# Gated down product: four of six rounds as seven half-size products; the gated entry in another row order

## What is computed

```
x = layer_norm(ALPHA * x + merged @ w_o, ln1_g, ln1_b)              # 1024 x 1024
hid = silu(x @ w_gate) * (x @ w_up)                                 # 1024 x 2816
x = layer_norm(ALPHA * x + hid @ w_down, ln2_g, ln2_b)              # 2816 x 1024
```

## Time and profile before

| | before |
|---|---|
| median of 3 runs | 2722.92 us (2715.91 to 2723.53) |
| the profiled execution | 2724.81 us, span 2722.9 us |
| matmuls (PE instructions) | 14122 |
| PE busy, DVE busy | 2608.5 us, 1756.0 us |
| mean granted clock of TensorE | 0.981 |

### The profile page before, as it was taken

The page is one execution under the profiler, slowest core; times in us unless marked ns, Lnnn a source line. Parts: engine busy times, 40 slices in busy tenths (PEclk is TensorE's granted clock), DMA queues, the critical chain, the costliest instruction groups (busy, mean ns, idle before and its releaser), DMA issues. The chain is left out here.

```text
span 2722.9 us, 35770 instructions
## 1 busy us (share of the span) xinstructions
PE 2608.5 (96%) x14122; PEld 2082.8 (76%) x14122; DVE 1756.0 (64%) x2663; ACT 902.2 (33%) x1578; POOL 479.2 (18%) x237
## 2 busy tenths in 40 slices
PE   7999999999899999999999999999969999999998
PEld 5875558884478887788888888868967888887887
DVE  5894997772667668999683355323276666666446
ACT  4334443420354544333231222232143322323121
POOL 1212644420000003333211121234200000000000
PEclk9999998989999999999999999999989999999999
DMA  4011032230133336333221222252322322235221
GB/s 160 31 63 67 31 124 94 95 125 23 62 109 113 110 111 243 105 102 108 89 90 51 75 87 69 71 208 70 124 78 64 91 77 86 78 93 224 76 110 62
DMA packets 192757, 262.22 MB, mean 96 GB/s; under 512 B 15952, under 2 KB 121808, under 8 KB 192208
## 3 DMA queue, kind: packets, MB, share of 16 engines
q1 hardware_dynamic: 192592, 259.95, 28.2%
HBM read 196.80 MB, written 61.93 MB: 95 GB/s over the span
## 5 line engine op out<-in xcount | busy, mean ns | idle before, releaser
L1341 PE MATMUL ps<-gl_t,gl_slot 128*128 128x512 f32 x1056 | 243.0, 389 | 0.0
L1341 PEld LDWEIGHTS ps<-gl_t,gl_slot 128*128 128x128 f32 x1056 | 198.3, 188 | 41.3
L1341 PE MATMUL ps<-gl_b,gl_slot 128*128 128x512 f32 x768 | 182.4, 395 | 18.4 <-DVE gl_slot L3912 18.4
L1341 PEld LDWEIGHTS ps<-gl_b,gl_slot 128*128 128x128 f32 x768 | 146.7, 191 | 49.9 <-issue 14.4
L1341 PE MATMUL ps<-ff_t,slot 128*128 128x512 f32 x768 | 179.2, 393 | 4.4 <-DVE ff_t L3195 4.4
L1341 PE MATMUL ps<-H_hi,tw_hi 128*128 128x512 f32 x448 | 175.6, 392 | 0.0
L1341 PE MATMUL ps<-H_rest,tw_hi 128*128 128x512 f32 x448 | 174.4, 389 | 0.0
L1341 PE MATMUL ps<-H_hi,tw_lo 128*128 128x512 f32 x448 | 174.3, 389 | 0.0
L1341 PEld LDWEIGHTS ps<-ff_t,slot 128*128 128x128 f32 x768 | 145.9, 190 | 35.3 <-DVE ff_t L3195 4.8
L1415 PE MATMUL ps<-wq_raw,H_plain 128*128 128x512 f32 x384 | 166.6, 593 | 2.6 <-ACT sb L2099 2.6
L1349 PE MATMUL ps<-b_hi,a_hi 128*128 128x512 f32 x376 | 147.3, 392 | 5.7 <-DVE sb L3535 3.8
(11 more groups left out here) (459 smaller groups left out, 5997.3 us busy)
## 6 DMA issues: line engine op xcount, KB each, us to landing
wraw<-in_w_ff SPq DMA_DIRECT2D x16, 1024.0 KB, 5.9
ff_raw<-ff_rows SPq DMA_DIRECT2D x8, 2048.0 KB, 8.0
slab_raw<-in_w_ff SPq DMA_DIRECT2D x16, 1024.0 KB, 5.0
ff_rows<-quad SPq DMA_DIRECT2D x61, 256.0 KB, 2.0
traw<-in_w_in SPq DMA_DIRECT2D x28, 512.0 KB, 4.4
wq_raw<-in_w_in SPq DMA_DIRECT2D x6, 2048.0 KB, 9.3
wraw<-in_w_gate SPq DMA_DIRECT2D x22, 512.0 KB, 3.9
wraw<-in_w_up SPq DMA_DIRECT2D x22, 512.0 KB, 5.1
```

The lines of the kernel that those rows point to most:

```text
L1341: mm = nc.tensor.matmul(out_ap, stationary(a, k), moving(c, k), start=(k == 0 and n == 0), stop=(k == kts - 1 and n == 2))
```

## The change

Rounds 1 to 4 of the gated down product (numbered r = 8 to 11 in the shared code) become seven half-size products each, with the functions of the first down product, which now take either stage. Round 0 (two contraction tiles) and the last round keep 16 outputs. DVE's sums t1, t2, t4 and the rests of products 0 and 1 of r = 8 stand among the additions of round 0; POOL makes the left sums of r = 8 and all left rests. The loads change places: the slabs of `w_down` for r = 8 are issued right behind rows 0 to 2 of X, those for r = 9 where those for round 1 stood, and the gain and shift of the last norm behind all of it. The entry's row order becomes 0 4 1 5 2 3 6 7, and the work on a transposed row moves from behind the norm of the row two later into it.

```diff
+LN_ROWS = (0, 4, 1, 5, 2, 3, 6, 7)
...
-            for i in range(GL_ROUNDS - 1):
-                for h in range(2):
-                    pe.wait_ge(v_lo, GL_ITEM_AT[("s", i, 1) if h else ("f", i, 3) if i else ("s", 0, 0)])
-                    for t in DOWN_ROWS:
-                        gl_output(i, h, t)
+            for h in range(2):
+                pe.wait_ge(v_lo, GL_ITEM_AT["s", 0, h])
+                for t in DOWN_ROWS:
+                    b = wait_bank(pe, *gl_down(0, h, t))
+                    split_product(ps[:, b, :], lambda a, k: (hid_lo if a else hid_hi)[:, k, t * P:(t + 1) * P],
+                                  lambda a, k: down_w[h][a][:, k, :], 2).then_inc(full[b], 1)
+            for r, x in GL_SEVENTH_ORDER:
+                seventh(r, x)
             pe.wait_ge(v_lo, GL_ITEM_AT["s", GL_ROUNDS - 1, 1])
...
                 if p == GL_PAIRS - 1 and x == 4:
                     gl_full(sp, p, x)
                     sp.dma_start(X[:, 0:3, :], xln_rows[0:3].rearrange("t p c -> p t c")).then_inc(part_in[0], 16)
+                    for h in range(2):
+                        gl_slab_load(GL_FIRST, h)
             sp.wait_ge(hid_f, 2 * GL_PAIRS - 1)
             sp.dma_start(X[:, 3, :], xln_rows[3]).then_inc(part_in[3], 16)
             for h in range(2):
                 sp.wait_ge(v_lo, GL_ITEM_AT["s", 0, h])
-                gl_slab_load(1, h)
+                gl_slab_load(GL_FIRST + 1, h)
...
             sp.dma_start(X[:, 6:NT, :], xln_rows[6:NT].rearrange("t p c -> p t c")).then_inc(part_in[6], 16)
+            quarter_full(sp, GL_FIRST, 0)
+            gl_hidden_load(GL_FIRST + 1)
+            for r in range(GL_FIRST + 2, GL_LAST + 1):
+                quarter_full(sp, r - 2, 4)
+                gl_slab_load(r, 0)
+                quarter_full(sp, r - 2, 3)
+                gl_slab_load(r, 1)
+                quarter_full(sp, r - 2, 6)
+                gl_hidden_load(r)
...
+            first_left_sums(GL_FIRST)
+            for x in FIRST_SEVEN[:6]:
+                left_rest(GL_FIRST, x)
+            for r in range(GL_FIRST + 1, GL_LAST):
+                later_left_rests(r)
...
-            for q, t in enumerate(MIX_ROWS):
+            for q, t in enumerate(LN_ROWS):
+                behind = LN_ROWS[q - 2] if q > 1 else None
                 merged_drain(t, 1)
                 for h in range(2):
                     wait_drained(dve, *merged("w", t, h))
                 row_mean(t)
+                if q > 1 and behind < 4:
+                    gl_rest_half(behind)
+                if q > 1 and behind >= 4:
+                    gl_term_sums(behind - 4)
+                    gl_rest_terms(behind - 4)
+                if q == NT - 1:
+                    gl_rest_weight(0)
+                    gl_rest_weight(1)
                 row_arg(t, q)
                 row_centred(t, q)
+                if q > 1 and behind >= 4:
+                    gl_rest_second(behind - 4)
                 row_root(t, 1)
                 row_normed(t, q)
-                if q > 1:
-                    gl_rest_turned(q - 2)
...
+            for h in range(2):
+                for t in DOWN_ROWS:
+                    b = wait_full(dve, *gl_down(0, h, t))
+                    xs = X[:, t, 512 * h:512 * h + 512]
+                    if h == 0 and t in (4, 0, 3, 6):
+                        dve.wait_ge(part_in[t], 64)
+                    V.scalar_tensor_tensor(xs, xs, ALPHA, ps[:, b, :], mul, add).then_inc(drained[b], 1)
+                    if (h, t) == (0, 1):
+                        right_sum(GL_FIRST, "t1")
+                    if (h, t) == (0, 3):
+                        right_rest(GL_FIRST, 0)
+                    if (h, t) == (0, 7):
+                        right_sum(GL_FIRST, "t2")
+                    if (h, t) == (1, 5):
+                        right_sum(GL_FIRST, "t4")
+                    if (h, t) == (1, 1):
+                        right_rest(GL_FIRST, 1)
+            first_rounds(GL_FIRST)
+            for r in range(GL_FIRST + 1, GL_LAST):
+                later_rounds(r, gl_last_rest)
+            gl_last_rest("s", 1)
+            quarter_added(GL_LAST - 1, 6)
```

458 lines of the change are left out of this document (257 added, 201 removed).

## The result

The changed kernel takes **2689.12 us** (median of 4 runs, 2687.22 to 2695.23), the kernel before, run beside it, 2720.66 us (2715.91 to 2723.53): a ratio of 0.9892, 95% interval 0.9879 to 0.9904, so 31.5 us or 1.1% faster, well over the 0.3% that a measurement tells. The forecast was 2697.4 (2688 to 2709). The median lies inside the range, 1.1 us above its lower end; the forecast gain was 25.5 us, so the change gave 6 us more than forecast. The other 2.3 us between 2697.4 and 2689.12 come from the kernel before, whose median was 2722.92 when the forecast was made.

A forecast was written before the change was run, and what follows sets the result against it. The prediction took PE's matmuls plus the few places where PE waits as the bound. Its terms, -21.8 for matmuls, +10.1 for start-up and -13.8 for the entry, summed to -25.5 us: median 2697.4 us, range 2688 to 2709.

The forecast's parts named there:

- Fewer matmuls: Four rounds of the gated down product: 168 matmuls each in place of 192, 96 fewer on PE's path, -21.8 us.
- DVE in the four rounds: Gated down product: DVE's 35.4 us a round fit under PE's 38.1, so its added work costs nothing.
- The rule against: DVE and POOL lock a shared SBUF port; six full 2.4 us blocks a round would give 49.8 us, time about 2744.
- rival D: Four rounds: each of POOL's six operations stretches DVE by 2.2 us, DVE becomes the bound, slower at 2739; chance 3%.
- The load of rows 6 and 7: Round 0 of the gated down product: X's load lands 2.6 us later, PE gap 3.7 us, bounds 1.0 and 6.3.
- Before product 1: Gated down product's round 0: DVE's list behind the load delays product 1, gap 2.7 us, bounds 0 and 6.5.
- First of the four rounds: Gated down product's first seven-product round: gaps like the first down product's opening, 4.0 us, bounds 1.5 and 6.
- Clock: Gated down product's start: PE loses 3.4 us to the lower clock level, bounds 0 and 5.2.
- Start-up together: Gated down product: load, product 1, first seven-round and clock sum to 13.7 us against 3.65 before, +10.1 us.
- The entry: Gated entry: new row order and DVE work moved into waits start PE's first term product at 2042.4, not 2056.17, -13.8 us.
- B: Gated down product: the start-up eats the saving, leaving a gain of 1.5 there, time 2707.6 us; chance 11%.
- C: Gated entry gives nothing because PE or ACT, not DVE, holds the rows; only -11.7, time 2711.2 us; chance 5%.

The follow-up runs named there:

- POOL behind: Against the changed kernel, POOL's six rests a round start 1.8 us later in the three later seven-product rounds, none added; 2710.63 us, ratio 0.9968.
- doubled: Against the changed kernel, 17 POOL subtractions of 2.4 us each added in the three later seven-product rounds; 2713.50 us, ratio 0.9975.

## Why the prediction was right, and where it was off

**Fewer matmuls, -21.8.** Right: x14026, and what is left of 229.87 - 217.9 is gaps and clock.

**DVE in the four rounds, nothing.** Right in its result (40.00 of 40 with DVE at 37.00), by luck in its sum. The prediction counted 28 additions and no meeting with POOL, 35.4 us a round. The later round read above has 24 additions (product 6 of a round and product 0 of the next are added up in the same banks and drained once), which is 2.4 us less, and three meetings of 0.65 us, which is 1.9 more: 35.13 measured. The two errors cancel, and so the cover, forecast at 2.7 us, was 3.0. Nor did the prediction have the reason why the meetings are cheap. It took 0.63 us as the price of meeting, and it is a price of timing: POOL is released by the first of four PSUM additions, 0.76 us into 2.4 us that it doesn't disturb, and no more than 0.8 us of its operation are left when DVE's next SBUF operation starts. Released 1.8 us later, the same operations made the down product 23 us longer.

**The rule against.** The rows above agree with it, more than the prediction gave it. The Trainium skill (SBUF — State Buffer, section "SBUF: two separate sides") has whichever of the two engines starts first hold the shared pair for its whole instruction and the other block; here a blocked DVE operation ended 1.07 to 1.09 us after POOL's end each time. What it left to the reader is when they meet, and that decides between 0.65 and 2.1 us. My estimate by it, 2744, took six full blocks in four rounds; the runs with POOL behind or doubled, in three rounds, came to 2711 and 2714. So rival D's mechanism is real and one wait away in this kernel; its long form (2.2 us a meeting, six a round) is what the run with POOL behind shows.

**The load of rows 6 and 7: +2.6, gap 3.7.** DVE could go on 4.2 us later against round 0's start (24.1, before 19.9), gap 5.62. The step that failed is the price: I counted bytes ahead of the load, and not that its condition, the write of the hidden pair, goes through the same queue and went from 4.6 to 9.92 us. The load itself took less than before, 9.09 us against 10.66. With the second pair behind it the load landed 3.0 us sooner.

**Before product 1: 2.7.** Was 0.54. From the landing (2469.75) to product 1 (2481.09) it took 11.3 us, and the forecast had 11.7 (2491.8 to 2503.5): DVE's list was priced well. But PE came to product 1 later. Its 36 matmuls from the end of the long gap took 10.0 us (2470.59 to 2480.55) and not 8.2, at the lower clock. So 1.6 us stood in this term and in the clock's, and were counted twice; with DVE the bound they cost PE nothing.

**First of the four rounds: 4.0.** Was 0.78 + 2.33 = 3.1, the same two gaps as in the first down product (1.48 and 2.36 there).

**Clock: 3.4.** Was 1.6, after the one long gap, and 1.1 us of the remainder aren't placed.

Start-up together 12.0 us (229.87 - 217.9) instead of 13.7, against 4.1 before (243.8 - 239.7) instead of 3.65: +7.9 where I had said +10.1. The down product gave 13.9, not 11.7.

**The entry: -13.8.** Was -16.5. The path was right to a microsecond. Against the anchor, with the 7.2 us taken off, the rows carrying terms took 9.9 us (10.1 forecast), those carrying a half 5.7 (5.75), the first gl_b matmul stood at 2015.63 (2016.3), PE's long piece at 2036.00 (2035.2). The step that failed is what it was compared with: 2056.17 was called PE's first product of the turned terms, and it is the fourth unit on gl_b, 12 matmuls ahead of them. Those took 5.2 us at the lower clock (2056.17 to 2061.38). Like for like the prediction's own 2042.4 meant 19.0 us; 18.2 came, of which 1.7 went back to the clock, a cost that the prediction didn't have.

So the sum was short by 2.7 at the entry and 2.2 in the down product; the other 1.1 of the 6 us lies within the spread of the runs. Both misses have one sign, and they left the median near the range's lower end; that it stayed inside owes something to luck. B and C didn't happen: no gap stands in a later round, and the entry gave more than its term.

## What to carry to other kernels

Two engines that block each other, as DVE and POOL do here on SBUF, don't cost each other a fixed sum. Release the one when the other turns to work that isn't disturbed, and look for operations that end a constant time after the other engine's end. To price a path that is cut differently by two versions, find the same instruction in both, by its operands and count, and only then subtract. A gap that gets shorter isn't yet time gained: look whether the product behind it starts earlier. Where DVE's list is cut into groups that each free one product's banks, balance the groups, since one long group stalls PE however early DVE arrives; and before an operation is moved forward, look when its data lands, for all that is queued behind it waits too.

## What the runs showed that I had not expected

The anchor, with the same code ahead of it in all but the two kernels that change the first down product, stood between 1961.65 and 1970.74 in the profiled executions: 9 us of spread that belongs to no change, over half of the gain at the entry. Between before and the changed kernel 1.6 of the 7.2 us are there by 386 us and 5.6 by 453 us. Between the two PE's granted clock is lower in the trace of before (0.83, 0.74 and 0.92 from 400 to 420, 440 and 460 us, against 0.91, 0.83 and 1.00); what lowered it isn't known. Differences of a few microseconds are better read from a stretch with the same first and last instruction: the entry stretch repeats within 0.8 us over the eleven kernels with the new entry, and the two profiles of the changed kernel agree on it to 0.01 us. The down stretch is less steady: 229.87 and 231.05 in the same two profiles, where the clock and the load's gap (5.62 us, or 1.75 and 4.85) differ.
